# A bias table on 128 partitions, strip transfers with stride 8, and compression weights in one transfer

## The reference

```python
gidx = cmp_start[:, None] + jnp.arange(NSA_CMP_LEN)[None, :]            # 15 windows of 32 positions, stride 16
kc = jnp.einsum('bnlgd,lde->bnge', k_cmp[:, gidx] + cmp_pe[:, None, :], cmp_wk)
vc = jnp.einsum('bnlgd,lde->bnge', v_cmp[:, gidx] + cmp_pe[:, None, :], cmp_wv)
...
s = jnp.einsum('bqgrd,bkgd->bgrqk', qb, kwb) * scale
s = s + rel_tab[rel_bucket(dist)].transpose(2, 3, 0, 1)                 # bias by distance, 16 heads
p = masked_softmax(s, valid)
```

## Time and profile before

| | us |
|---|---|
| median of 3 runs | 1127.42 |
| lowest and highest | 1122.23, 1129.05 |
| the profiled execution | 1130.25 |
| its span, first to last instruction | 1128.5 |

### The profile page before, as it was taken

The page is one execution under the profiler, slowest core; times in us unless marked ns, Lnnn a source line. Parts: engine busy times, 40 slices in busy tenths (PEclk is TensorE's granted clock), DMA queues, the critical chain, the costliest instruction groups (busy, mean ns, idle before and its releaser), DMA issues.

```text
span 1128.5 us, 21157 instructions
## 1 busy us (share of the span) xinstructions
PE 1053.8 (93%) x8292; PEld 1006.9 (89%) x8292; DVE 761.5 (67%) x1163; ACT 517.8 (46%) x904; POOL 4.7 (0%) x14
## 2 busy tenths in 40 slices
PE   5969988999999999999999999998988899999996
PEld 4968768899999989989999999998966889999995
DVE  3735885677777656666477777756674568767784
ACT  2324764544444445454363444445541445555552
POOL 0100000000000000000000000000000000000000
PEclk9988999999999999979999999999965899999998
DMA  9995656188889736602368888862630425655651
GB/s 321 260 274 161 222 201 251 51 313 305 305 299 314 258 112 236 231 19 76 112 222 302 304 303 306 292 246 87 212 112 1 134 91 194 203 179 171 224 183 38
DMA packets 62841, 229.22 MB, mean 203 GB/s; under 512 B 7064, under 2 KB 7320, under 8 KB 62392
## 3 DMA queue, kind: packets, MB, share of 16 engines
q1 hardware_dynamic: 62000, 225.69, 57.8%
q0 software_dynamic: 640, 2.10, 1.3%
q10 hardware_dynamic: 136, 0.52, 0.3%
HBM read 226.72 MB, written 1.57 MB: 202 GB/s over the span
## 4 chain that ended last, share of the span: by engine, by line
PE 77%; DVE 9%; DMA 6%; ACT 4%; issue 2%; SPq 1%; DVEq 0%; ACTq 0%
PE bank L1654 21%; PE bank L1655 21%; PE bank L1656 21%; DMA raw<-in_weights 2%; DVE acc L552 2%; DMA acc<-in_mod_w 2%; PE bank L1680 2%; PE bank L1671 2%; PE bank L1672 2%; DMA modbuf<-in_mod_w 1%; PE bank L2278 1%; DVE otok L1135 1%; PE bank L1742 1%; DVE wL L1081 1%; DVE hL L1129 1%
## 5 line engine op out<-in xcount | busy, mean ns | idle before, releaser
L1654 PE MATMUL bank<-hH,wH 128*128 128x256 f32 x1576 | 453.8, 288 | 12.2 <-DVE hL L1129 10.9
L1655 PE MATMUL bank<-hL,wH 128*128 128x256 f32 x1576 | 448.4, 285 | 0.0
L1656 PE MATMUL bank<-hH,wL 128*128 128x256 f32 x1576 | 448.2, 284 | 0.0
L1081 DVE TENSOR_TENSOR wL<-raw,wH 128x1024 fp32r<-128x1024 f32 x273 | 326.3, 1222 | 148.6 <-ACT wH L727 148.0
L1654 PEld LDWEIGHTS bank<-hH,wH 128*128 128x128 f32 x1576 | 304.8, 193 | 19.6 <-issue 15.0
L727 ACT ACTIVATE wH<-raw 128x1024 fp32r<-128x1024 f32 x273 | 273.4, 1049 | 97.9 <-PE bank L1656 61.1
L1655 PEld LDWEIGHTS bank<-hL,wH 128*128 128x128 f32 x1576 | 305.0, 194 | 0.2
L1656 PEld LDWEIGHTS bank<-hH,wL 128*128 128x128 f32 x1576 | 304.9, 193 | 0.0
L1654 PE MATMUL bank<-aH,wH 128*128 128x256 f32 x560 | 160.7, 287 | 2.1 <-DVE aL L1262 2.1
L1655 PE MATMUL bank<-aL,wH 128*128 128x256 f32 x560 | 160.0, 286 | 0.0
L1656 PE MATMUL bank<-aH,wL 128*128 128x256 f32 x560 | 159.7, 285 | 0.0
(11 more groups left out here) (295 smaller groups left out, 1129.2 us busy)
## 6 DMA issues: line engine op xcount, KB each, us to landing
raw<-in_weights SPq DMA_DIRECT2D x273, 512.0 KB, 4.7
modbuf<-in_mod_w SPq DMA_DIRECT2D x83, 512.0 KB, 5.1
modbuf<-in_w_ada SPq DMA_DIRECT2D x48, 512.0 KB, 5.1
strips<-bias_table POOLq DMA_DIRECT2D x8, 256.0 KB, 14.7
otok<-in_cmp_w SPq DMA_DIRECT2D x4, 512.0 KB, 11.5
raw<-in_mod_w SPq DMA_DIRECT2D x2, 512.0 KB, 5.3
otok<-in_mod_w SPq DMA_DIRECT2D x2, 512.0 KB, 10.0
sn<-in_mod_w SPq DMA_DIRECT2D x2, 512.0 KB, 13.7
```

Source lines behind the costliest of these rows:

```text
L1081: V.tensor_tensor(wL[:, slot, :], raw[:, slot, :], wH[:, slot, :].bitcast(F32), ALU.subtract).then_inc(lo_ready[c], 1)
L1654: mm(out, lhs_h, rhs_h, start=start, stop=False, skip_group_check=True)
L1655: mm(out, lhs_h, rhs_l, start=False, stop=False, skip_group_check=True)
L1656: return mm(out, lhs_l, rhs_h, start=False, stop=stop, skip_group_check=True)
```

## The change

The table is built on all 128 partitions by the matmul (16 copies of 8 slots, signs and masks as two more rows of the constants), ACT copies it out of the two banks and writes it as 128 rows of 4 KB. The shift per partition moves from this write to the strips' reads, and transfer a of the strips fills partitions a, a + 8, ... , a + 120, in the order 0, 4, 1, 5, 2, 6, 3, 7. Each of the two compression weight loads becomes one transfer from a source repeated twice in front.

```diff
-    rel = np.zeros((REL, 3 * 512), np.float32)
-    rel[rel_bucket(far), np.arange(512)] = 1.0
...
+    rel = np.zeros((REL + 2, 768), np.float32)
+    rel[rel_bucket(far), np.arange(512)] = -1.0
+    rel[REL, 0:512] = far < 0
+    rel[REL + 1, 0:512] = far >= 128
...
-            for g in range(G):
-                sp.dma_start(cw[g * HD:(g + 1) * HD], A["cmp_w"][0]).then_inc(cw_landed, 16)
+            sp.dma_start(cw, bcast(A["cmp_w"][0].unsqueeze(0), (G, HD, CLEN, HD))).then_inc(cw_landed, 16)
...
-                    for g in range(G):
-                        sp.dma_start(cw[g * HD:(g + 1) * HD], A["cmp_w"][1]).then_inc(cw_landed, 16)
+                    sp.dma_start(cw, bcast(A["cmp_w"][1].unsqueeze(0), (G, HD, CLEN, HD))).then_inc(cw_landed, 16)
...
-            for a in range(P // COPIES):
-
-                diag = bass.AP(A["table"].tensor, 2 * (P - COPIES * a), [[8 * ROW, COPIES], [ROW, 8], [1, 2 * S]])
-                pool.dma_start(strips[COPIES * a:COPIES * (a + 1)].rearrange("p a s j -> p a (s j)"),
-                               diag).then_inc(strips_landed, 16)
+            for a in (0, 4, 1, 5, 2, 6, 3, 7):
+
+                diag = bass.AP(A["table"].tensor, 2 * (P - 1 - a),
+                               [[8 * 1024 - 2 * 8, COPIES], [1024, 8], [1, 2 * S]])
+                pool.dma_start(strips[a:P:8].rearrange("p a s j -> p a (s j)"), diag).then_inc(strips_landed, 16)
...
+            act.wait_ge(misc_psum, misc["table"] + 1)
+            for n in range(2):
+                nc.scalar.activation(pt[:, n, :], bank[n][:, :], ACT.Copy).then_inc(misc_taken if n else table_half, 1)
+            act.wait_ge(table_half, 1)
             act.wait_ge(misc_taken, misc["table"] + 1)
-
-            shifted = bass.AP(A["table"].tensor, 2, [[ROW, 8], [8 * ROW + 2, COPIES], [1, 1024]])
-            act.dma_start(shifted, pt[0:8].rearrange("p a b -> p (a b)").unsqueeze(1).broadcast_to((8, COPIES, 1024))).then_inc(table_out, 16)
+            act.dma_start(A["table"], pt[:, :, :].rearrange("p a b -> p (a b)")).then_inc(table_out, 16)
...
-            jobs_upto(2)
-            take("table")
-            dve.wait_ge(rel_landed, 16)
-            for n in range(2):
-                ins = V.scalar_tensor_tensor(out=pt[0:8, n, :], in0=bank[n][0:8, :], scalar=-1.0,
-                                             in1=rel[0:8, 512 * (n + 1):512 * (n + 2)], op0=ALU.mult, op1=ALU.add)
-                if n == 0:
-                    link(ins)
-            taken(ins)
...
             for half in range(2):
-                out = bank[half][0:8, :].rearrange("p (n j) -> p n j", j=2)
+                out = bank[half][:, :].rearrange("p (n j) -> p n j", j=2)
                 for j in range(2):
-                    last = mm(out[:, :, j], param("reltab", REL)[:, 8 * j:8 * j + 8],
-                              rel[:, half * S:(half + 1) * S], start=True, stop=True, skip_group_check=True)
+                    last = mm(out[:, :, j], rel[:, 512 + j * P:512 + (j + 1) * P], rel[:, half * S:(half + 1) * S], start=True, stop=True,
+                              skip_group_check=True)
...
-                pe.wait_ge(cw_landed, 32 * (n + 1))
+                pe.wait_ge(cw_landed, 16 * (n + 1))
...
+    heads_of = np.concatenate([a["rel_table"], np.full((1, 16), BIG, np.float32),
+                               np.repeat(np.float32([[0.0, BIG]]), 8, 1)], 0).reshape(REL + 2, 8, 2)
+    rel[:, 512:] = np.tile(heads_of.transpose(0, 2, 1)[:, :, None, :], (1, 1, COPIES, 1)).reshape(REL + 2, 2 * P)
...
-    aps["table"] = nc.dram_tensor("bias_table", (COPIES, 8, ROW), F32, kind="Internal").ap()
+    aps["table"] = nc.dram_tensor("bias_table", (P, 1024), F32, kind="Internal").ap()
```

More of the change, by code:

```diff
@@ L44 @@
 COPIES = 16
-ROW = 1088
 RING = 6
@@ L72 @@
 _c = 0
-for _name, _n in (("c", 2 * KT), ("modb", 6 * 24), ("normw", 11 * KT), ("reltab", 16), ("relblock", 32),
+for _name, _n in (("c", 2 * KT), ("modb", 6 * 24), ("normw", 11 * KT), ("relblock", 32),
                   ("sinks", H), ("pe", CLEN), ("wga", KT * 24), ("gout", 8), ("gqk", 2),
@@ L249, in build_program @@
         ttf = tt.rearrange("p k s -> p (k s)")
-        rel = strips[0:REL, 0:3, :, :].rearrange("p a s j -> p (a s j)")
+        rel = strips[0:REL + 2, 0:2, :, :].rearrange("p a s j -> p (a s j)")[:, 0:768]
         hot_cmp = proj[:, 9:13, :].rearrange("p a s -> p (a s)")
@@ L267, in build_program @@
         cw_landed = sem("cw_landed")
+        table_half = sem("table_half")
         table_out = sem("table_out")
@@ L2380 @@
     put("bs", np.repeat(bs.transpose(1, 0, 2), HD, 0).reshape(P, -1))
-    put("reltab", a["rel_table"].reshape(REL, 8, 2).transpose(0, 2, 1).reshape(REL, 16), REL)
     blk = np.zeros((4, REL, 4, H), np.float32)
```

## The result

| | before | after |
|---|---|---|
| median, us (range, runs) | 1128.0 (1122.2 to 1129.1, 4) | 1145.6 (1142.4 to 1147.3, 4) |
| profiled execution: time, span, us | 1130.3, 1128.5 | 1147.3, 1145.5 |

The ratio after to before is 1.0163, 95% interval 1.0121 to 1.0206: 17.6 us slower. The forecast was 1145.

The account below looks back on a forecast made before the run. PE, busy 93% of the span, was taken to bound the kernel. Terms -0.6 + 1.2 + 14.8 + 2.5 = +17.9 us on the median of 1127.42 gave 1145, bounds 1134.9 to 1149; 0.80 between 1134 and 1157.

Parts of the forecast that it names:

- Two engines: Compression weight loads: the common outer cut of 2 leaves 1.05 MB to two engines, 25.6 GB/s each, 20.5 us.
- half of the count: Queue packets: one closing packet per engine used, engines following the outermost dimension; POOL's 128 left, 16 per strip transfer.
- The second load: Second compression weights, issued at 93.82 us: lands at 116.4, delaying PE and VectorE by 14.0 to 15.1 us, taken as +14.8.
- The clock term: After PE's 16 us idle for the second weights, a lowered clock costs +2.5 us, bounds 0 and 3.1.
- The first load and the stall: First weights ahead of units 7 and 8, stall up to 78.85 us: unit 8 at 77.3 against 76.1, +1.2 us.
- rival A: The forecast itself: both weights loads on two engines, strips twice as fast; 1145 us, bounds 1134.9 to 1149, chance 0.70.
- The table write: Start of the kernel: table written by 16 engines instead of 8, net -0.6 us, bounds -2.26 and +1.6.
- The +1.6: Start of the kernel: the constants' load of 34 rows runs on 2 engines, 52 KB each for 12, +1.6 us.
- Strips: Strip transfers on every eighth partition: 230 GB/s instead of 116, so 9.1 us instead of 18.1.
- Rival B: Broadcast load spreads over 16 engines, stall up to 78.85 us goes, decided from 4 engines on; 1113 us, chance 0.13.
- C: Weights loads: the broadcast spreads, but the strips stay slow; only -0.6 and -1.8 are left, 1125 us, chance 0.07.
- D: Weights loads on two engines and the strips stay slow: 1154 us, chance 0.10.

Follow-up runs that it names:

- outer 2 without a zero stride: The changed kernel with the weights stored as two blocks of 64 rows with a gap, nothing repeated: 1150.6 us, ratio 1.026 against the kernel before.
- 48 rows: The changed kernel with weights stored as 128 rows on the host, and the constants loaded as 48 rows instead of 34: 1109.5 us, ratio 0.986.
- The copied source: The changed kernel with the weights stored twice in memory as 128 rows, one transfer per load without zero stride: 1110.6 us, ratio 0.987.
- with four engines: The changed kernel with the weights' source stored as four blocks of 32 rows with gaps: 1142.3 us, ratio 1.018 against the kernel before.

## Why the prediction was right, step by step

The total was right to 1 us, but not each term.

1. *Two engines.* Right as put: share 0.13, two closing packets for each load, and outer 2 without a zero stride did the same. The rate was 52 to 54 GB/s for the pair, 26 to 27 for one engine, against the 25.6 worked out from 410 over 16. On POOL's queue every transfer had an outer 16 and 16 closing packets in all runs, so that half of the count was not tested.
2. *The second load* was mis-sized a little: 24.68 us from issue to landing against 22.6. By the packet records its data run from 97.33 to 120.24 us, 22.9 us and not 20.5: an 8 KB packet takes 309 ns from 110 us on, but up to 650, one 945, while units and modulation blocks run beside it up to 106 us. Only 1.8 us lie ahead of and behind the data, where I had counted 2.1. That 2.1 rests on a misreading, too: the 6.9 us of the earlier trace rows's load run from the second of its two issues, at 94.34, so it landed at 101.24 and not at 100.7. PE's move from the issue on is 19.5 - 2.2 = 17.3 us against 15.1. The clock term was 2.5, and 21.0 - 19.5 = 1.5 was measured at 126 us: of the 6.1 us behind the wait the granted clock was 0.73, not 0.57 as in the earlier trace rows.
3. *The first load and the stall* was the largest miss. The +1.2 is a place against the old trace (77.3 against 76.1), with the start's -0.6 already in it, so the sum counts that -0.6 twice; relative to the start it is +1.8. Measured are 3.9 against the old trace and 8.4 relative to the start (4.5 + 3.9), above the +2 of rival A's bounds, which no working backs. The place of the load was right: its first packet came at 48.99 us, and the strips' 9.1 us from their start at 39.0 + 1.2 give 49.3. Its rate was not: the data took 28.1 us (to 77.1) instead of 20.5, since beside strips, units and modulation blocks its 8 KB packets took 309 to 646 ns. I had priced them as if nothing ran beside them. So the first unit landed at 78.80 us. Units 7 and 8 came together, and a second split (1.2 us) stood ahead of the gates' copy. The mechanism held: with the first load alone broadcast the stall is 17.1 us, with the second alone there is none.
4. *The table write* was mis-sized the other way and fell outside its bounds: 4.5 us earlier and not 0.6. I had counted the shortage at 19 to 24 us alone. It goes on to 27 us (306 GB/s against 416 now), which makes 0.83 MB in all, on eight engines 4.0 us each by the same working and not 2.2. The block behind the one of the earlier trace rows, which VectorE takes at 27.94 us, now comes at 22.08; PE leads by 3.6 us at 29 us. The rest is clock: PE idled ahead of it, its granted clock was 0.50 at 27 to 30 us, and is 1.00 now. That the eight engines are the cause is argued: the same edit also took VectorE's two operations out of its order (its block behind them comes at 11.77 us instead of 14.75, but the lead is down to 0.6 by 19 us) and made the constants smaller, and no run parts these. The +1.6 for 34 rows on two engines was about right: 48 rows give 1.2 back.
5. *Strips.* 230 GB/s was assumed; at 44 to 47 us all queues together moved 231, and the last strip landed 15.1 us sooner after its issue.

So -4.5 + 8.4 - 1.7 + 17.3 + 1.5 = +21.0 at 126 us (the -1.7 between the stall and the next issue, 2.2 against 3.9, was not in the prediction), 0.3 more up to 162 us and 4.3 less later, is +17.0. The prediction had -0.6, +1.2, +14.8 and +2.5, +17.9. Two terms were 4 and 7 us off in opposite directions: that the total fits is in part luck.

Rival B named what the change would give if the load spread: 1113 us. The copied source does that, and by its ratio of 0.987 it would be 1112 on the forecast's median. B's condition was wrong, though: it has the stall gone from four engines on, and with four engines PE still stood 12.0 us there. C and D are out, since the strips did get faster: with them slow beside the broadcast, and the old table, 1166.7 us were measured, more than D's 1154.

## What to carry to other kernels

Look at a transfer's outermost dimension on both sides before joining two into one: it sets how many DMA engines carry the load. Here 2 in front gave two engines, as a broadcast or not, 4 gave four, 34 rows two, and 48 or 128 rows 16. More engines need not be faster, if they walk through partitions 32 apart. The price is paid where a queue is in order and the load stands before work on the critical path; a share of DMA time of k/16 beside a standing engine is its sign in a trace. When terms of a sum go both ways, test them one at a time: here two errors of 4 and 7 us cancelled in part.

## What the runs showed of the hardware

- On the queues of SyncE and ScalarE a transfer leaves one more packet for each engine that it used (136 and 144 on ScalarE's with 128 of data; 61928, 61932 and 61956 on SyncE's for two, four and 16 engines). A landing time is printed for the transfers on 16 engines, like the 48 rows (5.9 us), and not for those on two, four or eight.
- One engine of a pair moved 26 to 27 GB/s while the other 14 had nothing to do: idle engines take over nothing. Four engines on partitions 32 apart moved 17.5 each, and 26 each on the unit behind.
- The same 8 KB packet took 309 ns alone and up to 646 ns beside other transfers, so a load on two engines took 28.1 us instead of the 19.8 that 53 GB/s make.
- A full DMA share does not mean a full rate: 1.00 went with 116 GB/s while strips went to 16 neighbouring partitions, 1.03 with 419 at the start of the changed kernel.
- With the old table, read from eight partitions by eight engines, the queues moved 306 to 320 GB/s at 19 to 27 us, with the new one 416 to 419. Which of the two counts, the partitions or the engines, no run shows.
